# Two gated tiles transposed together, and the last pair's blocks in other raw slots, in a Strassen-like feed-forward of an encoder kernel

## The reference, cut to what matters

```python
D_MODEL, SEQ, DEPTH, D_FF = 1024, 256, 2, 2816          # one sequence, float32
for l in range(DEPTH):
    x = x + 0.5 * swiglu(rms_norm(x, ffn1_norm[l]), ffn1_w_gate[l], ffn1_w_up[l], ffn1_w_down[l])
    z = rms_norm(x, mix_norm[l]) @ w_in[l]              # q, k, v of 8 heads and p of 4 pooling groups
    x = x + concat([attention(q, k, v, rpb[l]), pool(p)]) @ w_out[l]
    x = x + 0.5 * swiglu(rms_norm(x, ffn2_norm[l]), ffn2_w_gate[l], ffn2_w_up[l], ffn2_w_down[l])
return rms_norm(x, final_norm)
# swiglu(h, g, u, d) = (silu(h @ g) * (h @ u)) @ d
```

## Time and profile before

| | us |
|---|---|
| median of 3 runs | 906.63 (906.47 to 907.05) |
| the profiled execution | 907.61 |
| its span, first to last instruction | 906.0 |
| PE busy | 896.7 (99%) |
| PEld busy | 731.4 (81%) |
| DVE busy | 774.1 (85%) |
| ACT busy | 569.6 (63%) |
| POOL busy | 57.5 (6%) |
| mean DMA rate | 204 GB/s |
| mean granted TensorE clock | 0.998 of 2.4 GHz |

### The profile page before, as it was taken

The page is one execution under the profiler, slowest core; times in us unless marked ns, Lnnn a source line. Parts: engine busy times, 40 slices in busy tenths (PEclk is TensorE's granted clock), DMA queues, the critical chain, the costliest instruction groups (busy, mean ns, idle before and its releaser), DMA issues.

```text
span 906.0 us, 11513 instructions
## 1 busy us (share of the span) xinstructions
PE 896.7 (99%) x4169; PEld 731.4 (81%) x4169; DVE 774.1 (85%) x1006; ACT 569.6 (63%) x821; POOL 57.5 (6%) x86
## 2 busy tenths in 40 slices
PE   8999999999999999999999999999999999999997
PEld 6788888787778888888788888887877888888885
DVE  5999998969757899898888998987787488999896
ACT  7865665567638766665586656564675496565653
POOL 1010101110001010101010101011100001010100
PEclk9999999999999999999999999999999999999999
DMA  7969777575245778786267878767534276877651
GB/s 254 356 149 317 200 263 180 139 264 188 93 135 191 279 187 277 187 278 163 94 233 277 216 249 216 249 151 210 201 141 142 90 260 219 241 227 236 215 157 46
DMA packets 135336, 185.11 MB, mean 204 GB/s; under 512 B 7793, under 2 KB 111521, under 8 KB 135281
## 3 DMA queue, kind: packets, MB, share of 16 engines
q1 hardware_dynamic: 117744, 165.43, 53.7%
q0 software_dynamic: 14208, 15.42, 10.5%
q10 hardware_dynamic: 3328, 3.54, 1.3%
HBM read 183.30 MB, written 2.07 MB: 205 GB/s over the span
## 4 chain that ended last, share of the span: by engine, by line
PE 96%; DMA 2%; DVE 1%; issue 1%; ACT 0%; POOLq 0%; ACTq 0%; SPq 0%; POOL 0%; DVEq 0%
PE ps L1519 29%; PE ps L1522 28%; PE ps L1520 28%; PE ps L1628 2%; PE ps L1602 1%; DMA w_raw<-in_w_in_dram 1%; PE ps L1529 1%; PE ps L1580 1%; PE ps L1530 1%; PE ps L1813 1%; PE ps L1829 1%; PE ps L1841 1%; PE ps L1858 1%; PE ps L1801 0%; PE ps L1867 0%
## 5 line engine op out<-in xcount | busy, mean ns | idle before, releaser
L1080 DVE TENSOR_TENSOR w_lo<-w_raw,w_hi 128x1024 fp32r<-128x1024 f32 x104 | 122.2, 1219 | 14.9 <-ACT w_hi L703 14.2
L1519 PE MATMUL ps<-w_hi,gt_hi 128*128 128x512 f32 (+1 forms) x322 | 126.1, 392 | 0.1
L1520 PE MATMUL ps<-w_lo,gt_hi 128*128 128x512 f32 (+1 forms) x322 | 125.0, 388 | 0.0
L703 ACT ACTIVATE w_hi<-w_raw 128x1024 fp32r<-128x1024 f32 x88 | 88.2, 1051 | 57.3 <-PE ps L1522 50.9
L1519 PE MATMUL ps<-w_hi,xt_hi 128*128 128x512 f32 x272 | 110.1, 405 | 0.1
L1520 PE MATMUL ps<-w_lo,xt_hi 128*128 128x512 f32 x272 | 106.2, 390 | 0.0
L1091 DVE SCALAR_TENSOR_TENSOR w_lo<-w_raw,gains,w_hi 128x512 fp32r<-128x512 f32 x128 | 88.0, 746 | 18.2 <-ACT w_hi L710 16.0
L1522 PE MATMUL ps<-w_hi,xt_lo 128*128 128x512 f32 x272 | 101.1, 391 | 0.0
L1522 PE MATMUL ps<-w_hi,gt_lo 128*128 128x512 f32 (+1 forms) x322 | 99.3, 388 | 0.0
L710 ACT ACTIVATE w_hi<-w_raw,gains 128x512 fp32r<-128x512 f32 x120 | 76.6, 714 | 9.2 <-DMA w_raw<-in_w_in_dram 4.8
L1519 PE MATMUL ps<-w_hi_f,xs_hi 128*128 128x512 f32 x192 | 75.9, 395 | 0.0
(11 more groups left out here) (166 smaller groups left out, 1882.5 us busy)
## 6 DMA issues: line engine op xcount, KB each, us to landing
w_raw<-in_ffn_w_gate_dram SPq DMA_DIRECT2D x54, 512.0 KB, 4.0
w_raw<-in_ffn_w_up_dram SPq DMA_DIRECT2D x54, 512.0 KB, 5.1
w_raw<-in_ffn_w_down_dram SPq DMA_DIRECT2D x48, 512.0 KB, 4.5
w_raw<-in_w_in_dram SPq DMA_DIRECT2D x32, 512.0 KB, 5.6
w_raw_f<-in_ffn_w_down_dram SPq DMA_DIRECT2D x24, 512.0 KB, 4.6
w_raw_e<-in_ffn_w_gate_dram SPq DMA_DIRECT2D x16, 512.0 KB, 5.4
w_raw_e<-in_ffn_w_up_dram SPq DMA_DIRECT2D x16, 512.0 KB, 6.4
w_raw_f<-in_ffn_w_gate_dram SPq DMA_DIRECT2D x16, 512.0 KB, 6.0
```

The lines of the kernel that those rows point to most:

```text
L703: nc.scalar.activation(w_hi[slot][:, part], w_raw[raw][:, part], ACT.Copy).then_inc(hi_ready[slot], 2)
L1080: nc.vector.tensor_tensor(w_lo[slot][:, part], w_raw[raw][:, part], w_hi[slot][:, part].bitcast(F32), ALU.subtract).then_inc(lo_ready[slot ...
L1519: nc.tensor.matmul(o, hi, wh, start=start, stop=False)
L1520: nc.tensor.matmul(o, hi, wl, start=False, stop=False)
```

## The change

Three things. (1) In the raw slots, B11.2 and B21.2 of the last pair change places: B21.2 is loaded into role d behind T4.1's split, B11.2 into role b behind 8b's. The last pair's fourth sum therefore lies in role d, and role b is free once the third addition (T4's, counted by sum_ready) is made. (2) SP no longer waits for the split of T4.2 at the end of a stage's list but for that third addition; only the load of the next stage's second unit waits for T4.2's split (last_sum_split). The final gain, which is loaded in the last stage, moves to role b's raw likewise. (3) Between pairs, x's four transposes no longer stand between the halves of the ordinary chunk; x's and y's are done in one group in the middle of its second half, x's in PSUM bank 6, y's in bank 7 (BANK_X), and y's no longer wait for x's low part. ACT makes both high parts behind B21 and DVE both low parts behind d{y} and B21. ACT's silu of the ordinary chunk, which writes the silu tile again, first waits for the third gate_pair.

```diff
-            b=("0b", "1b", "B12.0", "d4", "d5", "8b", "B21.2"),
-            d=("d0", "d1", "d2", "5b", "B21.1", "B11.2"),
+            b=("0b", "1b", "B12.0", "d4", "d5", "8b", "B11.2"),
+            d=("d0", "d1", "d2", "5b", "B21.1", "B21.2"),
...
-        final_gain = w_raw[FF2["d"]][:, 0:D_MODEL]
+        final_gain = w_raw[FF2["g"][1]][:, 0:D_MODEL]
...
+            def last_sum_split(layer, ff):
+                slot, n = split_of(layer, ff, "T4.2")
+                sp.wait_ge(lo_ready[slot], 4 * n + 5)
...
                     for h in range(2):
+                        if (ff, i, h) == (FF1, 0, 1):
+                            last_sum_split(layer - 1, FF2)
...
                 split("T4.1")
-                gate_up("B11.2", 10, 0)
+                gate_up("B21.2", 10, 1)
...
                 split("8b")
-                gate_up("B21.2", 10, 1)
+                gate_up("B11.2", 10, 0)
...
                 down(10)
-                split("T4.2")
+                summed(2, 3)
...
             def load_mix(layer):
                 for j in MIX_LOADS:
                     slot = MIX_SLOTS[j]
+                    if j == 1:
+                        last_sum_split(layer, FF1)
...
 # ACT, ff_body
                 unit(f"d{y}", (down_used, down_no(layer, ff, o + 2)))
-                store_gt_hi(layer, ff, x, 1)
+                act.wait_ge(pair_gated, 4 * n + 3)
                 silu_of(layer, ff, j + 3, 0)
                 unit(f"B21.{j + 1}", (m_ready, 7 * n + 7))
-                store_gt_hi(layer, ff, y)
+                store_gt_hi(layer, ff, x, 1)
+                store_gt_hi(layer, ff, y, bank=BANK_X)
...
 # DVE, ff_body
                 gate_pair(u, gated, 1, 1, 4 * n + 4)
-                store_gt_lo(layer, ff, x, 1)
                 unit(layer, ff, f"d{y}")
                 unit(layer, ff, f"B21.{j + 1}")
-                store_gt_lo(layer, ff, y)
+                store_gt_lo(layer, ff, x, 1)
+                store_gt_lo(layer, ff, y, bank=BANK_X)
...
 # PE
+            def transpose_pair(layer, ff, j):
+                transpose_x(layer, ff, j)
+                pe.wait_ge(pair_gated, 4 * pair_no(layer, ff, j) + 4)
+                transpose_tiles(gated, BANK_X)
...
                     ordinary(layer, ff, j + 2, 0, o)
-                    transpose_x(layer, ff, j - 1)
                     pe.wait_ge(combined, 7 * n + 6)
-                    ordinary(layer, ff, j + 2, 1, o, {4: lambda: transpose_y(layer, ff, j - 1)})
+                    ordinary(layer, ff, j + 2, 1, o, {4: lambda: transpose_pair(layer, ff, j - 1)})
```

More of the change, by code:

```diff
@@ L772, in first_norm, with store_gt_hi @@
                 act.wait_ge(gains_stored, 2)
-            def store_gt_hi(layer, ff, i, buf=0):
+            def store_gt_hi(layer, ff, i, buf=0, bank=6):
                 act.wait_ge(gt_ready, gt_no(layer, ff, i) + 1)
-                nc.scalar.activation(gt_hi[:, buf, :, :, :], ps[:, 6, :], ACT.Copy
+                nc.scalar.activation(gt_hi[:, buf, :, :, :], ps[:, bank, :], ACT.Copy
                                      ).then_inc(gt_hi_ready, 1)
@@ L1143, in gate, with store_gt_lo @@
                                                ).then_inc(gated_ready[t], 1)
-            def store_gt_lo(layer, ff, i, buf=0):
+            def store_gt_lo(layer, ff, i, buf=0, bank=6):
                 dve.wait_ge(gt_hi_ready, gt_no(layer, ff, i) + 1)
                 nc.vector.tensor_tensor(
-                    gt_lo[:, buf, :, :, :].rearrange("p k t q -> p (k t q)"), ps[:, 6, :],
+                    gt_lo[:, buf, :, :, :].rearrange("p k t q -> p (k t q)"), ps[:, bank, :],
                     gt_hi[:, buf, :, :, :].rearrange("p k t q -> p (k t q)").bitcast(F32),
@@ L1623, in seventh, with transpose_tiles @@
                 last.then_inc(m_ready, 1)
-            def transpose_tiles(source):
+            def transpose_tiles(source, bank=6):
                 for t in range(TT):
                     for k in range(2):
-                        last = nc.tensor.transpose(ps[:, 6, (k * TT + t) * P:(k * TT + t + 1) * P],
+                        last = nc.tensor.transpose(ps[:, bank, (k * TT + t) * P:(k * TT + t + 1) * P],
                                                    source[:, t, k * P:(k + 1) * P], ident[:, :])
```

## The result

| | before | after |
|---|---|---|
| median, us | 906.84 (906.47 to 907.20, 4 runs) | 918.41 (916.58 to 919.57, 4 runs) |
| profiled execution, its span, us | 907.61, 906.0 | 916.58, 914.8 |
| PE, ACT and DVE busy, us | 896.7, 569.6, 774.1 | 899.0, 569.0, 774.3 |
| granted TensorE clock of the span | 0.998 | 0.998 |

What follows compares the result with a forecast made beforehand. The prediction took TensorE's matmuls, busy 99% of the span, as the bound. Stops 6.5, less 1.15 for the boundary and 0.1 for the joining, gave +5.3 us: 906.63 + 5.3 = 911.9 us, range 909.5 to 914.5.

Steps and rivals of the forecast that it cites:

- Where and by what: Ahead of whole_down(x), first bodies: four TensorE stops released by DVE's gt_lo, ACT's B21 held by B21.1's load; +6.5 us.
- The joining: Between pairs: transposing x's and y's tiles in one group saves 0.01 us a body, 0.08 in all, nothing.
- Second bodies: At whole_down(x), j = 1: 1.4 us left, no stop, 0 us; rival that they stop too, 914 to 918, chance 0.05.
- The boundary: Start of layer 1's mixer: early load removes the residual wait, gain 1.15 us once; rival that it stays, 913.1, chance 0.08.
- first term: Ahead of whole_down(x), first bodies: stops of 1.85, 1.60, 1.45 and 1.62 us, slow restart of 0.11 included.
- second term: TensorE's clock behind the stops: forecast without a fall; a fall at each stop was a rival, chance 0.04.
- The rival: Behind each stop of 1.5 to 1.9 us the clock drops, costing 1.5 us more each: 918, chance 0.04.

Runs made afterwards that it cites:

- e4: Changed kernel with B21.1's load cut to a quarter of its rows, so its output is not the reference's: 909.30 us, ratio 1.0022.
- s2: Changed kernel with DVE alone making both tiles' low parts ahead of B21, ACT's order as in the changed kernel: 910.99 us, ratio 1.0041.
- s1: Changed kernel with ACT alone making both tiles' high parts ahead of B21, DVE's order as in the changed kernel: 936.37 us, ratio 1.0326.
- e3: Changed kernel, transposes still joined, with both tiles' high and low parts ahead of B21 on ACT and DVE: 906.26 us, ratio 0.9991.
- e1: Changed kernel with x's and y's tiles transposed and split where they were before, leaving only the slots and early load: 906.64 us, ratio 0.9994.
- r1: Changed kernel run once more, nothing edited: 917.49 us, ratio 1.0114.
- b1: e3 with the last pair's transposes moved inside runs of matmuls, and y's gating and high part moved earlier: 904.35 us, ratio 0.9967.
- b2: b1 again, unaltered, in another session: 904.14 us, ratio 0.9967.
- e2: Kernel before with only the joined transposes and their places on ACT and DVE, slots and loads as before: 919.43 us, ratio 1.0136.
- d2: e3 with three added sums on DVE ahead of x's low part in first bodies: 919.88 us, ratio 1.0143.
- d3: Changed kernel with two added sums on DVE ahead of x's low part in first bodies: 933.81 us, ratio 1.0293.

## Why the prediction was wrong

- **Where and by what (right).** Four stops ahead of whole_down(x), in first bodies only, released by gt_lo, with ACT held by B21.1's load. The chain from B21's high part to TensorE's restart was put at 4.18 us without the slow second matmul and measured 4.18 four times. That the load bounds it and not DVE's queue is shown by e4 (stops of 0.61 to 0.69), that it enters through ACT by s2, and that DVE's place behind B21 lets it in as well by the last stage of s1.
- **The joining (right).** Forecast to gain nothing: e3 has the joined transposes and stands at 0.9991 [0.9982, 1.0000], with the slots' edit in it.
- **Second bodies (right).** 1.4 us of room forecast, and about 1.6 found. s1 shows what that room hangs on: as long as DVE has B21 ahead of the tiles, ACT must have it ahead of them too.
- **The boundary (right in place, size not settled).** The gap of 0.93 us and the 0.22 us of slower transposes are gone in after and e1. Forecast 1.15; e1's profiled span is 1.1 us shorter than before's, one execution of each; the medians of e1 give 0.5 us (its interval reaches from a gain of 1.4 to a loss of 0.3), so it can't be told from 1.15 nor from nothing.
- **The failed step, first term: the size of a stop.** I put the stops at 1.74, 1.49, 1.34 and 1.51 us and the slow restart of 0.11; they were 1.82, 2.10, 1.84 and 2.36: 2.0 us more. B21.1's second half accounts for 1.8 of that: in after it took 0.03, 0.55, 0.45 and 0.81 us longer than in before. I read "nothing in the diff touches it" as "it takes as long as in before", and no run bears that out: in all ten profiles with joined transposes and the full load it takes longer from the second stage on, and in layer 1 (1.3 us of the 1.8) an instruction packet falls into it. In before this duration had no effect on the end, so one execution's value was all I had, and I gave it 0.3 us either way on all four. The six profiled executions in the table range from 4.92 to 6.60, and all of the load's length that forecast and range could have known of was the 4.94 to 5.28 of before. Each microsecond of it, once ACT's idle time is exposed to TensorE, is a microsecond of the end; r1 shows it twice in one kernel.
- **The failed step, second term: the clock.** I gave it 0.04 and treated it as all or none: either every stop drops the clock or none does. My one row against it was a gap of 0.93 us, little over half the length of the stops I forecast, and I let it speak for them. The clock fell once in after's profiled execution, for 1.6 us, and by their mean clocks one to three times in the others. This term hangs on the first: behind stops of the forecast length the runs show no fall (0 of 14 up to 1.94 us), behind the longer ones they do. The rival's 918 us is near the measured time by coincidence: it adds four falls to stops of 1.3 to 1.7 us; its price of 1.5 us for a fall is about right. Of the missing 6.3 us the profiled spans show 3.5: 2.0 from longer stops and 1.6 from the fall. Of the other 2.8, 0.8 is before's own spread, 1.8 after's and 0.2 lies outside the spans; the mean clocks and r1's loads put the 1.8 on the same two terms, but no profile shows it.
- **The range.** 914.5 as its upper end followed from the two errors. With 5.0 to 6.6 us for every load and none to three falls of 1.6 us the same sum reaches from about 912 to 923 (an estimate from after's stops).

## What to carry to other kernels

A piece of work on which the bounding engine will soon wait must not be queued behind one that waits for a load; look in the trace for the idle time before the unit ahead of it, even where that idle time is free today. If two engines handle the same two things one after the other, give both the same order, or each waits for what the other has put last (eight stops instead of four). And the duration of a transfer that was hidden is one sample: when an edit exposes it, size the stop by its spread over every execution and stage there is, look at what else the DMA engines carry in that moment, which an edit elsewhere can move, and add what a stop of the fastest engine costs afterwards.

## What the runs showed of the hardware

**A stop of TensorE can cost more than its length.** In the profiled executions of before, e1, e3, b1 and b2, with no stop in the bodies, the granted clock stays at its full level between the start and the end of the kernel. In the others:

| stop | number (kernels) | followed by a stretch at 1.2 GHz |
|---|---|---|
| 0.61 to 1.94 us | 14 (e4, s2, e2, after, r1) | 0 |
| 2.10 to 2.47 us | 14 (after, r1, d2, s1) | 7 |
| 2.82 to 4.82 us | 8 (e2, r1, s1, d3) | 8 |

Each stretch is 3.413 us long (three in d3 6.827). Read from the starts of the matmuls, each of the eleven outside d3 delays them by 1.6 to 1.7 us (in after the eleven spacings from 811.35 to 815.46 take 4.11 us instead of 2.5); in d3 it is 2.2 on average by the account of the span. Equal stops in one execution are followed by a fall or not (d2), so a kernel with stops of this length has a wider spread than one without: 3.0 us over four executions of after, 0.7 us over four of the kernel before. The Trainium skill (TensorE: Matmul & The Clock Gate, "HAM oscillation — how this bites in real kernels") describes waits between bursts of matmuls after which the next burst runs at half clock; these runs agree as to the direction; here stops of little over 2 us in an otherwise dense stream were enough in half of the cases, which is shorter than the waits of the page's case.

**The same load, at the same place in the same kernel, varies by over a microsecond** between executions in two sessions (5.39 and 6.60 us, after and r1), with the same loads asked for around it by the program. What differs is when the 16 KB packet of kind "instruction" began, 0.7 and 3.1 us after the asking; over 20 loads the later beginnings go with the longer loads (5.39 to 6.10 us up to 2.3 us, 6.36 to 6.61 us after that). As long as the load was hidden, nothing in the kernel's time told of it.
